# Running the gate and up products of the next expert ahead of the down product of this one, in a mixture-of-experts stage

## The reference, cut to what matters

```python
logits = jnp.einsum('btd,de->bte', h, w_r)
aff = jax.nn.softmax(logits, axis=-1)
gate, idx = lax.top_k(jnp.swapaxes(aff, 1, 2), cap)        # cap = 128
xe = jax.vmap(lambda hb, ib: hb[ib])(h, idx)
a = jnp.einsum('becd,edf->becf', xe, w_g)                  # 1024 -> 512
u = jnp.einsum('becd,edf->becf', xe, w_u)
ye = jnp.einsum('becf,efd->becd', jax.nn.silu(a) * u, w_d) * gate[..., None]
return zeros.at[idx].add(ye)                               # and x = x + g2 * this
```

## Time and profile before

| | |
|---|---|
| median of three timed runs | 2644.97 us (2643.72 to 2646.24) |
| the profiled execution's own time | 2644.1 us |
| its span in the profile | 2642.3 us |
| the experts' stage, from the first transposes of tokens to the end | 2295.4 to 2642.3 us |
| one expert in steady state | 20.47 us |

### The profile page before, as it was taken

The page is one execution under the profiler, slowest core; times in us unless marked ns, Lnnn a source line. Parts: engine busy times, 40 slices in busy tenths (PEclk is TensorE's granted clock), DMA queues, the critical chain, the costliest instruction groups (busy, mean ns, idle before and its releaser), DMA issues.

```text
span 2642.3 us, 28340 instructions
## 1 busy us (share of the span) xinstructions
PE 2344.8 (89%) x11580; PEld 1934.2 (73%) x11580; DVE 1474.8 (56%) x2132; ACT 1038.7 (39%) x1568; POOL 281.2 (11%) x368
## 2 busy tenths in 40 slices
PE   5999989999999999889899796899998897288886
PEld 4888868888888888668788485677776684167775
DVE  5676444445454544742312328377776535788886
ACT  4677323212221222321311123266666214177775
POOL 2111000001100110000000016300000101011120
PEclk9999989999999999899999798799999898599999
DMA  3124311233332432022221020100000704699993
GB/s 127 50 76 140 136 40 64 88 100 128 113 102 93 140 112 67 26 106 95 68 86 63 12 78 2 52 1 1 1 1 10 258 32 170 221 324 369 358 358 86
DMA packets 81027, 287.56 MB, mean 109 GB/s; under 512 B 10049, under 2 KB 10177, under 8 KB 79233
## 3 DMA queue, kind: packets, MB, share of 16 engines
q1 hardware_dynamic: 50256, 180.12, 19.1%
q0 software_dynamic: 30640, 105.63, 12.8%
HBM read 250.05 MB, written 35.65 MB: 108 GB/s over the span
## 4 chain that ended last, share of the span: by engine, by line
PE 72%; DVE 17%; ACT 7%; issue 2%; DMA 1%; POOL 0%; POOLq 0%; DVEq 0%; ACTq 0%
PE psum L98 22%; PE psum L99 22%; PE psum L100 22%; DVE small L2269 3%; ACT PB L2205 3%; DVE MP_lo L2306 2%; ACT MP_hi L2235 1%; PE psum L867 1%; PE psum L309 1%; PE psum L840 1%; DVE idx L2546 1%; DVE vals L2544 1%; DVE cur L2549 1%; DVE xe_lo L2697 1%; DMA gal<-gas 1%
## 5 line engine op out<-in xcount | busy, mean ns | idle before, releaser
L98 PE MATMUL psum<-U_hi,w_hi 128*128 128x512 f32 (+1 forms) x1216 | 481.3, 396 | 46.9 <-DVE w_lo L231 36.2
L99 PE MATMUL psum<-U_lo,w_hi 128*128 128x512 f32 (+1 forms) x1216 | 478.2, 393 | 0.0
L100 PE MATMUL psum<-U_hi,w_lo 128*128 128x512 f32 (+1 forms) x1216 | 477.7, 393 | 0.0
L222 ACT ACTIVATE w_hi<-raw 128x1024 fp32r<-128x1024 f32 (+3 forms) x177 | 177.6, 1007 | 381.3 <-PE psum L100 374.5
L231 DVE TENSOR_TENSOR w_lo<-raw,w_hi 128x1024 fp32r<-128x1024 f32 (+3 forms) x177 | 206.4, 1173 | 216.7 <-ACT w_hi L222 215.2
L98 PEld LDWEIGHTS psum<-U_hi,w_hi 128*128 128x128 f32 (+1 forms) x1216 | 230.1, 189 | 100.2 <-DVE w_lo L231 37.4
L100 PEld LDWEIGHTS psum<-U_hi,w_lo 128*128 128x128 f32 (+1 forms) x1216 | 229.6, 189 | 51.0 <-issue 0.8
L99 PEld LDWEIGHTS psum<-U_lo,w_hi 128*128 128x128 f32 (+1 forms) x1216 | 230.0, 189 | 47.6 <-issue 0.8
L98 PE MATMUL psum<-a_hi,w_hi 128*128 128x512 f32 x512 | 199.2, 389 | 0.0
L99 PE MATMUL psum<-a_lo,w_hi 128*128 128x512 f32 x512 | 199.2, 389 | 0.0
L100 PE MATMUL psum<-a_hi,w_lo 128*128 128x512 f32 x512 | 199.2, 389 | 0.0
(11 more groups left out here) (351 smaller groups left out, 4882.3 us busy)
## 6 DMA issues: line engine op xcount, KB each, us to landing
rawe<-in_w_e SPq DMA_DIRECT2D x112, 512.0 KB, 8.1
mraw<-in_w_mod POOLq DMA_DIRECT2D x128, 256.0 KB, 2.9
rawx<-in_w_e SPq DMA_DIRECT2D x56, 512.0 KB, 9.6
raw<-in_w_up SPq DMA_DIRECT2D x32, 512.0 KB, 3.6
raw<-in_w_dn SPq DMA_DIRECT2D x32, 512.0 KB, 3.6
raw<-in_w_e SPq DMA_DIRECT2D x24, 512.0 KB, 8.3
raw<-in_dft_t SPq DMA_DIRECT2D x16, 512.0 KB, 3.5
X<-in_xT SPq DMA_DIRECT2D x4, 1024.0 KB, 9.3
```

Source lines behind the costliest of these rows:

```text
L98: e.matmul(o, l[0], r[0], start=first, stop=False, skip_group_check=skip)
L99: e.matmul(o, l[0], r[1], start=False, stop=False, skip_group_check=skip)
L100: return e.matmul(o, l[1], r[0], start=False, stop=last, skip_group_check=skip)
L222: act.e.activation(w_hl[x.place][0][:, 0:x.width], w_raw[x.slot][:, 0:x.width], ACT.Copy).then_inc(w_hi, 1)
```

## The change

The PE's order is shifted by one expert. In step e it now does: gate and up of e+1, chunk 0; transposes of the hidden values of e; chunk 1; chunk 2; the transposes of the tokens of e+2; chunk 3; then the down product of e. ACT and DVE follow the same order. The banks of PSUM are now the same for all experts (2 for tokens, 1 each for gate and up, 1 for the turned hidden values, 2 for the down product). The output's scaling leaves DVE: ACT copies the down product out of PSUM, scaled by the gate, and POOL multiplies the result by g2 in SBUF (128x1024 float32) ahead of the scatter. POOL's order of gathers and scatters is as before. The stored order of the weights in memory is as before; they are loaded in the new order of use.

```diff
     def moe_pool(pool):
...
             if e_ < 14:
                 gather(pool, e_ + 2)
-            pool.wait_ge(*moe.dve("ye", e_))
+            pool.wait_ge(*moe.act("ye", e_))
+            pool.wait_ge(*rt.act("g2"))
+            pool.e.tensor_tensor(ye[i][:], ye[i][:], g2b[:], ALU.mult).then_inc(*moe.pool.one("ye", e_))
             if e_:
                 pool.wait_ge(*ye_out[1 - i].at((e_ + 1) // 2))
...
+            pool.wait_ge(*moe.pool("ye", e_))
             pool.e.indirect_dma_start(
...
     def moe_act(act):
...
+        act.wait_ge(*rt.pe("row", 7))
+        turn_in(0)
+        for c in range(4):
+            make_hi(act, T_G[0, c, 1] + 3)
+        turn_in(1)
+        silu(0)
+        for e_ in range(16):
+            for c in range(4):
+                if e_ < 15:
+                    make_hi(act, T_G[e_ + 1, c, 1] + 3)
+                if c == 0:
+                    act.wait_ge(*moe.pe("ht", e_))
+                    if e_:
+                        act.wait_ge(*moe.pe("down", e_ - 1, 3))
+                    act.e.activation(flat(hT[0]), bank(ht_b), ACT.Copy).then_inc(*moe.act.one("ht", e_))
+                if c == 2 and e_ < 14:
+                    turn_in(e_ + 2)
             if e_ < 15:
+                make_hi(act, T_D[e_, 0] + 3)
+                silu(e_ + 1)
+            for c in range(4):
+                make_hi(act, T_D[e_, c] + 3)
+            act.wait_ge(*moe.pe("down", e_, 3))
+            act.wait_ge(*rt.dve("gcol"))
+            if e_ > 1:
+                act.wait_ge(*ye_out[e_ % 2].at(e_ // 2))
+            act.e.activation(ye[e_ % 2][:], two(ye_b), ACT.Copy, scale=gcol[:, e_:e_ + 1]).then_inc(
+                *moe.act.one("ye", e_))
...
     def moe_dve(dve):
...
-            dve.wait_ge(*moe.pe("down", e_, 3))
-            dve.wait_ge(*rt.act("g2"))
-            dve.wait_ge(*rt.dve("gcol"))
-            if e_ > 1:
-                dve.wait_ge(*ye_out[i].at(e_ // 2))
-            dve.e.scalar_tensor_tensor(ye[i][:], two(ye_b[e_]), gcol[:, e_:e_ + 1], g2b[:], ALU.mult,
-                                       ALU.mult).then_inc(*moe.dve.one("ye", e_))
...
     def moe_pe(pe):
+        def turn_in(e_):
+            if e_:
+                pe.wait_ge(*moe.dve("xe", e_ - 1))
+            pe.wait_ge(*xg_in[e_ % 2].at(e_ // 2 + 1))
+            for k in range(8):
+                m = pe.e.transpose(two(xe_b)[:, k * P:k * P + P], xg[e_ % 2][:, k * P:k * P + P], ident[:])
+            m.then_inc(*moe.pe.one("turn", e_))
+
+        def gate_up(e_, c):
+            if c == 0:
+                pe.wait_ge(*moe.dve("xe", e_))
+                if e_:
+                    pe.wait_ge(*moe.act("silu", e_ - 1))
+                    pe.wait_ge(*moe.dve("hv", e_ - 1))
...
+        for c in range(4):
+            gate_up(0, c)
+        turn_in(1)
...
         for e_ in range(16):
...
             for c in range(4):
+                if e_ < 15:
+                    gate_up(e_ + 1, c)
+                if c == 0:
+                    pe.wait_ge(*moe.dve("hv", e_))
+                    if e_:
+                        pe.wait_ge(*moe.dve("ht", e_ - 1))
+                    for i in range(4):
+                        m = pe.e.transpose(bank(ht_b, i * P, i * P + P), hv[:, i * P:i * P + P], ident[:])
+                    m.then_inc(*moe.pe.one("ht", e_))
+                if c == 2 and e_ < 14:
+                    turn_in(e_ + 2)
+            pe.wait_ge(*moe.dve("ht", e_))
+            if e_:
+                pe.wait_ge(*moe.act("ye", e_ - 1))
             for c in range(4):
-                w = use(pe, T_E[12 * e_ + 8 + c])
+                w = use(pe, T_D[e_, c])
```

More of the change, by code:

```diff
@@ L2512, in router_act @@
             act.e.activation(row[r % 5][:], two(row_b[r]), ACT.Copy).then_inc(*rt.act.one("row", r))
-        make_hi(act, T_E[0] + 3)
+        make_hi(act, T_E0 + 3)
         act.wait_ge(*rt.pe("g2"))
@@ L2551, in router_dve @@
         e.tensor_copy(idxf[0:16, :], idx[0:16, :]).then_inc(*rt.dve.one("idxf"))
-        make_lo(dve, T_E[0] + 3)
+        make_lo(dve, T_E0 + 3)
         dve.wait_ge(*rt.pe("top"))
@@ L2609, in _program, with plan_gu, plan_turn @@
     ye_out = [Loads(sem(f"ye_out{i}")) for i in range(2)]
[L2610 to L2615, removed]
+    moe = Stage(sem, "moe")
+    xe_b, gu_b, ht_b, ye_b = next_banks(2), [next_banks() for _ in range(2)], next_banks(), next_banks(2)
+    T_G, T_D = {}, {}
+    T_E0 = len(tiles)
+    def plan_gu(e_, c):
+        for y in range(2):
+            moe.pe.plan(("gu", e_, c, y))
+            T_G[e_, c, y] = tile("w_e", 12 * e_ + 2 * c + y, moe.pe("gu", e_, c, y))
+    def plan_turn(e_):
+        moe.pe.plan(("turn", e_))
+        moe.act.plan(("xe", e_))
+        moe.dve.plan(("xe", e_))
+    plan_turn(0)
+    for c in range(4):
+        plan_gu(0, c)
+    plan_turn(1)
+    moe.act.plan(("silu", 0))
+    moe.dve.plan(("hv", 0))
     for e_ in range(16):
-        gu_b[e_, 0], gu_b[e_, 1] = next_banks(), next_banks()
         for c in range(4):
[L2619 to L2623, removed]
-        if e_ < 15:
[L2625 to L2633, removed]
+            if e_ < 15:
+                plan_gu(e_ + 1, c)
+            if c == 0:
+                moe.pe.plan(("ht", e_))
+                moe.act.plan(("ht", e_))
+                moe.dve.plan(("ht", e_))
+            if c == 2 and e_ < 14:
+                plan_turn(e_ + 2)
+        if e_ < 15:
+            moe.act.plan(("silu", e_ + 1))
+            moe.dve.plan(("hv", e_ + 1))
         for c in range(4):
             moe.pe.plan(("down", e_, c))
-            T_E.append(tile("w_e", len(T_E), moe.pe("down", e_, c)))
-        moe.dve.plan(("ye", e_))
+            T_D[e_, c] = tile("w_e", 12 * e_ + 8 + c, moe.pe("down", e_, c))
+        moe.act.plan(("ye", e_))
+        moe.pool.plan(("ye", e_))
     ring_a = [at(f"rawe{i}", [1024], O_V + 4 * i * KB) for i in range(15)]
@@ L2648, in _program @@
     w_in += [Loads(sem(f"ring_in{i}")) for i in range(23)]
-    place_tiles([(T_E[0] + k) % N_RAW for k in range(N_RAW)] + list(range(N_RAW, N_RAW + 23)), T_E[0], 2, T_Q[7] + 1)
+    place_tiles([(T_E0 + k) % N_RAW for k in range(N_RAW)] + list(range(N_RAW, N_RAW + 23)), T_E0, 2, T_Q[7] + 1)
     def weights_sp(sp):
@@ L2686, in flat, with silu @@
         return y[:].rearrange("p a b -> p (a b)")
-    def xe_act(act, e_):
-        act.wait_ge(*moe.pe("turn", e_))
-        if e_ > 1:
[L2691 to L2705, removed]
-    def moe_act(act):
[L2708 to L2712, removed]
+    def moe_act(act):
+        def turn_in(e_):
+            act.wait_ge(*moe.pe("turn", e_))
+            if e_ > 1:
+                act.wait_ge(*moe.pe("gu", e_ - 2, 3, 1))
+            act.e.activation(flat(xe[e_ % 2][0]), two(xe_b), ACT.Copy).then_inc(*moe.act.one("xe", e_))
+        def silu(e_):
             act.wait_ge(*moe.pe("gu", e_, 3, 0))
@@ L2715, in moe_act, with turn_in, times @@
                 act.wait_ge(*moe.dve("hv", e_ - 1))
-            act.e.activation(hs[:], bank(gu_b[e_, 0]), ACT.Silu).then_inc(*moe.act.one("silu", e_))
-            if e_ < 15:
[L2718 to L2724, removed]
-    def moe_dve(dve):
[L2727 to L2731, removed]
+            act.e.activation(hs[:], bank(gu_b[0]), ACT.Silu).then_inc(*moe.act.one("silu", e_))
+        act.wait_ge(*rt.pe("row", 7))
[15 more added lines that the diff above has]
+                    turn_in(e_ + 2)
+            if e_ < 15:
+                make_hi(act, T_D[e_, 0] + 3)
[4 more added lines that the diff above has]
+            act.wait_ge(*rt.dve("gcol"))
+            if e_ > 1:
+                act.wait_ge(*ye_out[e_ % 2].at(e_ // 2))
+            act.e.activation(ye[e_ % 2][:], two(ye_b), ACT.Copy, scale=gcol[:, e_:e_ + 1]).then_inc(
+                *moe.act.one("ye", e_))
+    def moe_dve(dve):
+        def turn_in(e_):
+            hi, lo = xe[e_ % 2]
+            dve.wait_ge(*moe.act("xe", e_))
+            dve.e.tensor_tensor(flat(lo), two(xe_b), f(flat(hi)), ALU.subtract).then_inc(*moe.dve.one("xe", e_))
+        def times(e_):
             dve.wait_ge(*moe.act("silu", e_))
@@ L2735, in moe_dve @@
                 dve.wait_ge(*moe.pe("ht", e_ - 1))
-            dve.e.tensor_tensor(hv[:], bank(gu_b[e_, 1]), hs[:], ALU.mult).then_inc(*moe.dve.one("hv", e_))
-            if e_ < 15:
[L2738 to L2743, removed]
-            dve.wait_ge(*moe.pe("down", e_, 3))
@@ L2745, in moe_dve @@
-            dve.wait_ge(*rt.act("g2"))
-            dve.wait_ge(*rt.dve("gcol"))
-            if e_ > 1:
-                dve.wait_ge(*ye_out[i].at(e_ // 2))
-            dve.e.scalar_tensor_tensor(ye[i][:], two(ye_b[e_]), gcol[:, e_:e_ + 1], g2b[:], ALU.mult,
-                                       ALU.mult).then_inc(*moe.dve.one("ye", e_))
-    def moe_pe(pe):
-        xe_pe(pe, 0)
+            dve.e.tensor_tensor(hv[:], bank(gu_b[1]), hs[:], ALU.mult).then_inc(*moe.dve.one("hv", e_))
+        turn_in(0)
@@ new lines, in moe_dve @@
+        for c in range(4):
```

(61 more changed lines are left out.)

## The result

The changed kernel takes 2743.64 us (2740.66 to 2746.68), the kernel before 2645.6 us in the same comparison: a ratio of 1.037, with a 95% interval of 1.0352 to 1.0388. It is 98 us slower; 2724 us was forecast, in a range of 2668 to 2762.

A forecast was written before the change was run, and what follows sets the result against it. PE, DVE and DMA were nearly full at 20.47 us an expert; the new bound was a chain through POOL, 15.6 + 9.0 landing + 2.1 clock = 26.7 us. 13 x period - 267 = +80 us: 2724 us, range 2668 to 2762.

The forecast's parts named there:

- the sum: Terms added up: gather issue 6.45 us after the down product, period 26.7 us, +80 us in all.
- The landing, L: From the gather's issue to its landing among weight loads: 9.0 us taken, bounds 4.3 and 10.7.
- The share of half the engines: Scatter issue to gather landing, 12.9 us, read as if the pair had half the DMA engines.
- The clock: PE idle 6 to 6.5 us per period lowers its clock three times in four: 2.1 us, bounds 0 and 2.8.
- The period: One down product's end to the next, through POOL: 15.6 + 9.0 = 24.6 us, 26.7 with clock falls.
- step 0: First expert's step: its gather is early, it ends at 2335.4 us, +0.5 us.
- step 15: Last expert's step: hidden values' transposes and down product, 7.6 us.
- The shared port: POOL's multiplication stops DVE up to 2.4 us per expert, covered by the gather wait; POOL waiting on DVE taken as 0.
- Fast landing: Rival: weight loads run dry, gather lands in 5.5 to 7.5 us; +20 to +30, about 2668 us; chance 0.14.
- The DMA floor: Rival: full DMA engines keep the period near 20.5 us, 2643 us; chance of no change 0.05.
- Everything adds: Rival: landing 10.7, port 1.2, clock 2.8 us; period 30.3 us, +127, 2771 us; chance 0.03.
- The chain closed inside the other work: Rival: gather lands as on an idle DMA, 4.3 us; period 19.9 us, -8, 2636 us; chance of faster 0.06.

## Why the prediction was right

The step that decided it held as written: gather e+2 leaves behind scatter e-1 and is wanted in step e, three chunks after the down product. From its end at 2452.96 to the gather's issue at 2459.46 it was 6.50 us, against 6.45 in the sum. That the sum came out so close is in part luck, since two single terms were off and cancelled: POOL waited 0.81 us and not 0.15 for its own multiplication's end, and the pair of issues took 2.07 and not 2.63.

**The landing, L**, was the term that was too small: 10.4 us in the median for 9.0. I had expected the loads to thin. From 2463 us to the landing the engines are full (1.03), so the gather shared them to the end. Leaving L at the 10.3 of the earlier trace rows would have been better than my correction of it. The share of half the engines predicts nothing by itself: it was fitted to that 10.3, and with the 2.07 us that the pair of issues now takes its 12.9 us would give 10.8. Weight loads and scatter are worth 3.1 us each when taken away alone, and 4.9 together.

**The clock** fell in twelve of the thirteen waits by the transposes' 1.97 us, more often than my three in four, and cost 2.15 us each time where I allowed up to 2.8. That is 2.0 a period for 2.1 in the sum, so here too the product was better than its factors.

**The period** was 1.3 us too short, 27.97 for 26.7, and this hides two errors of opposite sign. The first twelve periods, from one copy of the down product to the next, are 28.5 us in the mean: L brings 1.4 of the missing 1.8. In the thirteenth the gather landed in 5.6 us, with no weight load issued from 2684 us on, and the period was 21.45. The sum had no term for that; had the step been like the others, the kernel would have been some 7 us slower still, by my estimate from these two periods.

**The rest** of the sum, on the spans (2744.0 - 2642.3 = 101.7 us, +80 forecast): the period brings 13 x 1.3 = 17 us of the missing 22; step 0 ended at 2338.1 us for 2335.4, of which 0.7 us had come in ahead of the stage; step 15 took 9.8 us for 7.6, since a wait of 2.0 us for `hT_lo` there brought the clock down again; the end cost +2.4 for +2.1.

**The shared port**: POOL's multiplication stopped DVE, and the gather's wait covered it, as forecast. But a low part took 2.6 us in place of 1.22, a loss of 1.4, and not up to 3.6 with a loss of 2.4, as I had counted. I took 0 for POOL waiting on DVE; its multiplication took 2.40 us in nearly all experts, as with no wait. What the prediction had wrong is the price when the cover goes. I wrote that 18.9 us or a little more would be the floor, from busy time; with early gathers the period was 18.53 with POOL's multiplication and 17.69 without. And in the old order the hold cost some 30 us, although DVE had 1.6 us free in each period by the same busy times. I take it that the hold counts because it comes when only a few tiles are made ahead; no run tries that. The Trainium skill (SBUF — State Buffer, on the shared port pair) says that whichever of the two starts first has the pair for its whole instruction and the other is blocked. The trace agrees: the low part that began at 2482.63 us ended at 2485.23, 1.1 us behind the multiplication's end, which is about its own length.

**The rivals.** Fast landing: no, 5.6 us came only once, at the end of the loads. The DMA floor: no, 17.69 us was reached. Everything adds: no, L was 10.4 and the clock 2.15, and the port's 1.2 us didn't come. The chain closed inside the other work only in the kernels in which the gather landed in 5.5 us or left a turn earlier.

## What to carry to other kernels

When the order on one engine is shifted, follow every producer that isn't shifted with it, DMA issues by index above all: here the tokens were wanted a whole step sooner and still left behind the last step's result. Moving the gather alone made a 3.7% loss into a 0.9% gain. Before work goes from DVE to POOL, look at what DVE does at that moment: here an operation with two SBUF inputs on DVE stood still while POOL's ran, and 2.4 us on POOL cost more than the 1.28 us that it took off DVE (18.53 us a period for 17.69).

## What the runs showed of the hardware

- A short wait more can tip the clock. With PE waits of 0.84 and 1.5 us an expert the granted clock stayed at 1.00; with one of 0.7 us more, some 9 us ahead of them, it was 0.57 to 0.70 in the 4 us behind them in 7 of 13 experts, and 1.00 in the other six, with the same waits. Nor is the extra wait always needed: behind waits of 1.6 and 1.4 us in the first expert the clock stayed at 1.00 in the kernel before and fell to 0.57 in the one with the scaling on ACT and no multiplication. What decides was not tried.
- A fall of the clock behind a wait of some 7 us cost 2.15 us on the chain: 11.47 us from the transposes to the end of the down product, for 9.32 with the clock kept up.
- A DMA share of 1.0 was no sign of a floor: the kernel with the scaling on DVE and early gathers had 1.03 at a period 14% shorter, at 384 GB/s for 357, and the delay went into the loads' landing, 8 growing to 19 us, where it stayed at 5 to 10 in the kernel before.
- The issue of an indirect DMA on POOL isn't a constant. The same gather took 1.36 us in the kernel before, 1.95 in the changed one and 4.2 us in the one with early gathers and the scaling on DVE; scatters took 1.55 to 3.46. What sets it was not tried.
